# Modulation vectors of two transformer blocks: from VectorE sums to TensorE products in four column groups

## The reference

```python
# first block, layer l
ada = jax.nn.silu(c) @ w_ada[l] + b_ada[l]           # 1024 -> 6 * 1024
sh1, sc1, g1, sh2, sc2, g2 = jnp.split(ada, 6, axis=-1)
h = x * (1.0 + sc1) + sh1
y = mixer(h, ...)                                    # qkv, attention, w_o
x = layer_norm(ALPHA * x + (1.0 + g1) * y, ...)
h = x * (1.0 + sc2) + sh2
x = layer_norm(ALPHA * x + (1.0 + g2) * swiglu(h), ...)

# second block, layer l: two vectors from one matrix
mod_x = jax.nn.silu(c_2) @ w_ada_2[l] + b_ada_2[l]     # 1024 -> 9 * 1024
mod_c = jax.nn.silu(c_ctx_2) @ w_ada_2[l] + b_ada_2[l]
# swiglu half step, mixer, swiglu half step, each modulated and gated
```

## Time and profile before

| | |
|---|---|
| median of 3 runs | 2935.88 us (2933.57 to 2938.0) |
| the profiled execution | 2934.27 us |
| its span, first to last instruction | 2932.5 us |
| PE busy | 2669.5 us, 91% of the span |
| DVE busy | 1757.8 us, 60% |
| ACT busy | 1081.4 us, 37% |
| POOL busy | 224.9 us, 8% |
| read from HBM | 409.75 MB |
| mean granted clock of PE | 0.926 |

### The profile page before, as it was taken

How to read it: one execution, slowest core, us unless ns; L and a number is a source line. 1 busy time by engine, 2 the same in 40 slices (tenths; PEclk the granted TensorE clock), 3 DMA queues, 4 the chain that set the end, 5 groups by cost and what they waited for, 6 DMA issues and landing times. The chain is left out here.

```text
span 2932.5 us, 39627 instructions
## 1 busy us (share of the span) xinstructions
PE 2669.5 (91%) x15387; PEld 2241.6 (76%) x15387; DVE 1757.8 (60%) x3177; ACT 1081.4 (37%) x2061; POOL 224.9 (8%) x167
## 2 busy tenths in 40 slices
PE   4768998998998799998999889999899998988899
PEld 4747997867998588886855668888688886856899
DVE  6567776537776655545748566544655433647654
ACT  2343543433443323223326442322333322316553
POOL 2000100000100201101000020000111000100110
PEclk8867998967999899999989999999999999879999
DMA  8924774903676144332720134443244433720453
GB/s 287 279 84 144 254 255 130 270 29 102 232 243 200 51 150 144 126 122 83 214 72 1 44 100 130 137 133 119 93 145 135 138 120 116 214 72 24 142 178 133
DMA packets 355603, 413.91 MB, mean 141 GB/s; under 512 B 25707, under 2 KB 292628, under 8 KB 355352
## 3 DMA queue, kind: packets, MB, share of 16 engines
q1 hardware_dynamic: 353326, 404.37, 43.3%
q0 software_dynamic: 736, 4.58, 0.5%
q10 hardware_dynamic: 1354, 2.43, 0.2%
HBM read 409.75 MB, written 5.27 MB: 142 GB/s over the span
## 5 line engine op out<-in xcount | busy, mean ns | idle before, releaser
L640 DVE TENSOR_TENSOR weight_lo<-raw_weights,weight_hi 128x512 fp32r<-128x512 f32 x1024 | 778.1, 767 | 929.6 <-ACT weight_hi L1168 919.6
L1168 ACT ACTIVATE weight_hi<-raw_weights 128x512 fp32r<-128x512 f32 x1024 | 633.0, 629 | 1326.2 <-PE bank L845 1192.5
L845 PE MATMUL bank<-H_hi,weight_hi 128*128 128x256 f32 (+1 forms) x2832 | 975.0, 344 | 109.6 <-POOL H_lo L806 77.6
L845 PE MATMUL bank<-H_lo,weight_hi 128*128 128x256 f32 (+1 forms) x2832 | 956.4, 338 | 0.0
L845 PE MATMUL bank<-H_hi,weight_lo 128*128 128x256 f32 (+1 forms) x2832 | 956.4, 338 | 0.0
L845 PEld LDWEIGHTS bank<-H_hi,weight_hi 128*128 128x128 f32 x2832 | 558.0, 197 | 187.6 <-issue 112.6
L845 PEld LDWEIGHTS bank<-H_hi,weight_lo 128*128 128x128 f32 x2832 | 558.4, 197 | 50.7
L845 PEld LDWEIGHTS bank<-H_lo,weight_hi 128*128 128x128 f32 x2832 | 559.7, 198 | 48.7 <-issue 0.5
L1459 DVE SCALAR_TENSOR_TENSOR ada_partial<-raw_weights,silu_c,ada_partial 128x512 f32<-128x512 f32 x616 | 441.5, 743 | 1.3 <-DVE ada_partial L1459 0.2
L845 PE MATMUL bank<-hidden_hi,weight_hi 128*128 128x256 f32 (+1 forms) x1056 | 359.0, 340 | 3.8 <-DVE weight_lo L640 3.8
L845 PE MATMUL bank<-hidden_hi,weight_lo 128*128 128x256 f32 (+1 forms) x1056 | 354.1, 335 | 0.0
(11 more groups left out here) (165 smaller groups left out, 2124.4 us busy)
## 6 DMA issues: line engine op xcount, KB each, us to landing
raw_weights<-in_w_ada_dram SPq DMA_DIRECT2D x120, 1024.0 KB, 5.4
raw_weights<-in_w_ffn_up_dram SPq DMA_DIRECT2D x88, 1024.0 KB, 5.2
raw_weights<-in_w_ffn_in_dram SPq DMA_DIRECT2D x44, 1024.0 KB, 5.4
raw_weights<-in_w_ffn_down_dram SPq DMA_DIRECT2D x32, 1024.0 KB, 5.3
raw_weights<-in_w_in_dram SPq DMA_DIRECT2D x18, 1024.0 KB, 8.3
raw_weights<-in_w_ffn_out_dram SPq DMA_DIRECT2D x16, 1024.0 KB, 7.7
raw_weights<-in_w_in_ab_dram SPq DMA_DIRECT2D x12, 1024.0 KB, 9.4
raw_weights<-in_w_in_cd_dram SPq DMA_DIRECT2D x12, 1024.0 KB, 7.7
```

The source lines that it names most:

```text
L640: eng.tensor_tensor(WL[:, p.g % SPLIT, 0:p.kt * CW].rearrange("p (t n) -> p t n", n=CW), raw_ap(ch.n, ch.kt, CW)[:, p.k0:p.k0 + p.kt, :], ...
L845: return pe.matmul(o, w, x, start=start, stop=stop, skip_group_check=True)
L1168: act.activation(WH[:, p.g % SPLIT, 0:p.kt * CW].rearrange("p (t n) -> p t n", n=CW), raw_ap(ch.n, ch.kt, CW)[:, p.k0:p.k0 + p.kt, :], ACT ...
```

## The change

**PE does the products.** A chunk is used by PE alone: for each of its four row tiles one fp32 product with 512 moving columns of raw weights, straight from the slot. The stationary side is 32 columns wide, three conditioning vectors and 29 columns of zeros (`SILU_C`, now 128 by 8 by 32). Tile k writes partitions 32k to 32k + 31 of bank 7, so the four products of a chunk are in four column groups of the array. The second chunk of a group adds to the first.

**A group is then closed in three steps.** ACT copies the bank to `ada_sums` (`copy_sums`), at the second piece of the following main chunk. PE turns it by four transposes of 128 by 128 back into bank 7 (`turn_sums`), ahead of the last piece of that chunk. DVE adds the four partial sums by one small reduce and adds the bias (`join_sums`, `columns`), which counts `ada_out`. The first chunk of the next group waits for that count on PE.

**Chunks change places.** The first qkv hosts 8 instead of 12, the second 9 items instead of 8 (8 chunks instead of 7, since one item is not a main chunk), the third 7 instead of 8, and w_out of the second block's first layer 4 instead of none. Everything between is hosted four, later three, places later.

```diff
-        def ada(at, f):
-            close(f(at.u).raw_order)
-        def sum_rows(g):
-            nv = vectors(ADA[AG * g])
-            pe.wait_ge(ada_used, AG * (g + 1))
-            if g > 0:
-                pe.wait_ge(ada_out, g)
-            for j in range(AW // P):
-                for v in range(nv):
-                    ins = mm(B_ADA[:, j * nv + v:j * nv + v + 1],
-                             ACC[:, g % 2, v, j * P:(j + 1) * P], ones[:, 0:1], True, True)
-            ins.then_inc(ada_sum, 1)
+        def ada(ch):
+            wait_landed(pe, one, lambda _: ch)
+            g, first = ch.raw_order // AG, ch.raw_order % AG * AK
+            if first == 0 and g > 0:
+                pe.wait_ge(ada_out, g)
+            w = raw_ap(ch.n, AK, AW)
+            for k in range(AK):
+                ins = mm(B_ADA[32 * k:32 * k + 32, :], SILU_C[:, first + k, :], w[:, k, :], first == 0,
+                         first + k >= KC - AK)
+            ins.then_inc(ada_used, 1)
+            if first:
+                to_turn.append(g)
+        def turn_sums():
+            while to_turn:
+                g = to_turn.pop(0)
+                pe.wait_ge(ada_copied, g + 1)
+                for j in range(AW // P):
+                    ins = pe.transpose(B_ADA[:, P * j:P * j + P], ASUM[:, P * j:P * j + P], ident[:, :])
+                ins.then_inc(ada_sum, 1)
...
                 ins.then_inc(piece_used.sem, 1)
+                if i == len(ch.pieces) - 2:
+                    turn_sums()
...
+        def copy_sums():
+            while to_copy:
+                g = to_copy.pop(0)
+                act.wait_ge(ada_used, AG * (g + 1))
+                act.activation(ASUM[:, :], B_ADA[:, :], ACT.Copy).then_inc(ada_copied, 1)
...
-                    if first + k == 0:
-                        ins = dve.tensor_scalar(acc, w[:, k, :], SILU_C[:, i:i + 1], None, ALU.mult)
-                    else:
-                        chain.wait(closed["acc"][v])
-                        ins = dve.scalar_tensor_tensor(out=acc, in0=w[:, k, :], scalar=SILU_C[:, i:i + 1], in1=acc,
-                                                       op0=ALU.mult, op1=ALU.add)
...
+            parts = B_ADA[:, :].rearrange("p (c q r) -> p c r q", q=AK, r=32)[:, :, v0:v0 + nv, :]
+            chain.link(dve.tensor_reduce(APART[:, :, 0:nv], parts, AX.X, ALU.add))
+            dve.tensor_tensor(AD[m][:, n * at:n * at + n, 0:nv], APART[:, :, 0:nv],
+                              b[:, :, None].broadcast_to([P, n, nv]), ALU.add).then_inc(ada_out, 1)
...
 # proj, on DVE, after the eviction of a column group
                 dve.sem_inc(g.grp.tally.sem, 1)
+                join_sums()
+                if g.host:
+                    ada(g.host)
...
 # qkv, on DVE
-                    ahead_of(one, lambda _: it.chunk, (lambda _: it.host) if it.host else None)
+                    ahead_of(one, lambda _: it.chunk)
+                    join_sums()
+                    if it.host:
+                        ada(it.host)
...
-         (2816, ("v", 768))], T, 12, T, 0)
+         (2816, ("v", 768))], T, 8, T, 0)
...
-         (2560, ("v", 512)), (2816, ("v", 768))], T, 8, T, 1)
+         (2560, ("v", 512)), (2816, ("v", 768))], T, 9, T, 1)
...
-             (1280, ("k", 2)), (1536, ("v", 0)), (1792, ("v", 256)), (2048, ("kv",))], n, 8, T if last else n, 2 + l)
+             (1280, ("k", 2)), (1536, ("v", 0)), (1792, ("v", 256)), (2048, ("kv",))], n, 8 if last else 7, T if last else n, 2 + l)
...
-        w_out(a["w_out_2"][l], n2, 2 + l, 5, False, 0)
+        w_out(a["w_out_2"][l], n2, 2 + l, 5, False, 0 if last else 4)
```

More of the change, by code:

```diff
@@ L519, in qkv @@
         st.hosted = len(ADA)
+        assert st.hosted % AG == 0
         state.update(q_in=st.done, normed=None, hosted=st.hosted)
@@ L942, in qkv @@
                 if it.host:
-                    ada(one, lambda _: it.host)
-            if s.hosted:
-                close(s.hosted)
+                    ada(it.host)
+            turn_sums()
         def ffn_in(s):
@@ L1136, in _ @@
             elif s.kind == "ada":
+                pe.wait_ge(silu_done, 1)
                 for ch in s.chunks:
-                    ada(one, lambda _, ch=ch: ch)
-                close(s.hosted)
+                    ada(ch)
+                    turn_sums()
             elif s.kind in ("ln", "rms"):
+                turn_sums()
                 stats(s, before)
@@ L1200, in setup @@
             act.wait_ge(cols_done, 1)
[L1201 to L1204, removed]
+            for v in range(3):
+                ins = act.activation(SILU_C[:, :, v], C_COLS[:, 8 * v:8 * v + 8], ACT.Silu)
             ins.then_inc(silu_done, 1)
@@ L1263, in qkv @@
                     ahead(one, lambda _: p, split, late)
+                    if p is it.chunk.pieces[1]:
+                        copy_sums()
                 used(one, lambda _: it.chunk.pieces[-1])
@@ L1304, in step @@
                     ahead(at, lambda k: s.steps[k].u.pieces[i], split, late)
+                    if s.host and i == 1:
+                        ada(s.steps[at.u].host)
+                        copy_sums()
                 hidden_hi(at)
@@ L1397, in _ @@
             elif s.kind == "ada":
+                for ch in s.chunks:
+                    ada(ch)
+                    copy_sums()
                 flush()
@@ L1423, in _ @@
         late = list(range(SPLIT))
-        closed = {"read": 0, "acc": [0, 0]}
+        to_join = []
         one = At(None, 0, 1, 1)
@@ L1436, in used, with ada, ahead_of, join_sums @@
             dve.wait_ge(piece_used.sem, at(lambda s: f(s).g + SPLIT + 1))
[L1438 to L1454, removed]
-                    if first + k == 0:
-                        ins = dve.tensor_scalar(acc, w[:, k, :], SILU_C[:, i:i + 1], None, ALU.mult)
-                    else:
-                        chain.wait(closed["acc"][v])
-                        ins = dve.scalar_tensor_tensor(out=acc, in0=w[:, k, :], scalar=SILU_C[:, i:i + 1], in1=acc,
-                                                       op0=ALU.mult, op1=ALU.add)
[L1461 to L1469, removed]
-                ahead(at, lambda k: f(k).pieces[i], split, late)
[L1471 to L1477, removed]
+        def ada(ch):
+            if ch.raw_order % AG == AG - 1:
+                to_join.append(ch.raw_order // AG)
+        def ahead_of(at, f):
+            for i in range(len(f(at.u).pieces)):
+                ahead(at, lambda k: f(k).pieces[i], split, late)
+        def join_sums():
+            while to_join:
+                columns(to_join.pop(0))
         def columns(g):
@@ L1602, in step @@
                 dve.sem_inc(ev_dve.sem, 1)
[L1603 to L1606, removed]
-            else:
-                each(dve, 0, 10, 2, step)
-            step(At(None, 10, 1, 1))
+                if s.host:
+                    ada(s.steps[at.u].host)
+                    join_sums()
+            each(dve, 0, 11, 2, step)
         def proj(s):
@@ L1616, in proj @@
                 for ch in g.chunks:
-                    ahead_of(one, lambda _: ch, (lambda _: g.host) if g.host and ch is g.chunks[-1] else None)
+                    ahead_of(one, lambda _: ch)
                 used(one, lambda _: g.chunks[-1].pieces[-1])
@@ L1778, in _ @@
             elif s.kind == "ada":
+                lambdas()
                 for ch in s.chunks:
-                    ada(one, lambda _, ch=ch: ch)
-                    if ch is s.chunks[3]:
-                        lambdas()
-                close(s.hosted)
+                    ada(ch)
+                    join_sums()
                 flush()
```

46 lines of the change are left out of this document (26 added, 20 removed).

## The result

The changed kernel takes **3038.58 us** (median of 4 runs, 3035.18 to 3042.28), the kernel before, run beside it, 2936.94 (2933.57 to 2939.59): ratio **1.0347, 95% interval 1.0328 to 1.0366**, 101.6 us slower. The forecast was 3039.

A forecast was written before the change was run, and what follows sets the result against it. PE, 91% busy, was taken to bind most, with DVE's work mostly hidden. Terms 83 - 12 + 31 + 12 - 4 - 12 + 3 + 2 = +103 us on 2934.27 gave 3039 us (median 1.6 above); own range 2976 to 3065, stated range 2965 to 3090.

The forecast's parts named there:

- PE's price: Where PE is full: 1.2 us per chunk, 0.6 per group, +156 us; sum blocks leaving PE -73; net +83.
- Four groups side by side: Modulation products on PE: four column groups run fully side by side, as two do in attention; 1.06 us per block.
- The rival of two at a time: Modulation products on PE: pairs go one after the other, sum rises by 90 us to 3129; chance 0.09.
- Strict order: Rival: second records wait for first in PE's queue, four products take five record times; +135 us, 3174; chance 0.04.
- The new wait: PE waits for DVE's join: 3.7 and 4.0 us in projections (+31), 2.0 in qkv (+12), second qkv -4.
- eight projections ... +31: One wait of PE for the join in each of eight projections, 3.7 or 4.0 us each: +31 us.
- What DVE gives back: DVE loses its sums; gain is 2.2 us in each of 5.5 step pairs at 750 to 870 us: -12.
- Worth something only where DVE binds: DVE's relief counts at 750 to 870 us, -12, and in the second qkv at most 6.8 us.
- First qkv and setup: First qkv: -12 for three items without modulation, +3 for the nine before; setup +2, between -3 and +8.
- What would show it: Signs in the new trace, among them the first k,q product 10 us earlier than 160.96 and join waits of 43 to 60.
- ACT gets 60 copies ... hidden: ACT's 60 bank copies, 0.63 us each, are hidden, since ACT has 69 us of work in 140.
- Second qkv: Three join waits come where PE waited for pieces anyway (6.8 us); both put together at -4.

The follow-up runs named there:

- the experiment with two groups: Changed kernel with DVE's join one piece earlier (2970.84 us), a chunk's four products put in two column groups instead of four: 3050.95 us.
- the small one alone: Kernel before with only the four chunks moved and open groups closed behind each projection, sums still on DVE: 2911.24 us, ratio 0.9927.

## Why the prediction was right, step by step

- *PE's price.* Right where PE is fullest: 1.2 us per chunk against 1.23 in the up stages, measured by leaving the products out. Too high in the projections, 0.87. A pair of steps with 512 columns 1073.38 - 1026.90 = 46.48 against 46.5 forecast; with 256 columns and two vectors 785.13 - 759.25 = 25.88 against 26.0 (starts of two chunks' products, two steps apart).
- *Four groups side by side.* Shown. The rival of two at a time is the experiment with two groups, 80 us away; the 0.09 that it had was fair, since no row of the kernel before had shown more than two. Strict order fell too: the four first records start within 0.02 us (1166.254 to 1166.274), the second ones 0.45 later, and two records of one product take as long as eight of four. The estimate by the Trainium skill ("TensorE: Matmul & The Clock Gate", Part 3, measured speedup) of 1.08 us for the block is 0.08 above the 1.00 to the next main product.
- *The new wait.* Mechanism and place right, size wrong in one of two parts. The projections' waits, forecast at 3.7 and 4.0, are 3.6 to 3.9, eight of them; qkv's, forecast at 2.0, are 1.87 to 1.90; 53.4 us in all within 43 to 60. But I priced a wait at its own length: "eight projections ... +31" recovered 49.6 when it went. The clock behind the pause was missing, 18.4 us by the estimate above. The forecast for the projections holds all the same (55.4 against 59.5), since other terms there missed the other way.
- *What DVE gives back.* Half counted. "Worth something only where DVE binds", -12, was near for the second up stage (13.9 with the sums out, 10.4 of it behind the first 96 products), and left out 3.8 in the first w_out, 4.0 in the second down-projection, 5.6 in the first qkv and 7.5 in the setup. I read DVE's shortage in one stretch of the earlier trace rows and did not look at the stages next to it. Either half of the change alone gives the second up stage's gain of 7.8 or nearly so.
- *First qkv and setup.* Forecast -12 + 3 + 2, measured -5.0. The first k,q product moved from 160.96 to 156.9, by 4 us, not the 7 of these terms (the 10 under "What would show it" does not follow from them). The step that failed is "ACT gets 60 copies ... hidden": I argued it from stretches where the pieces were in place, and in this one the copy stood behind a rounding that waited for its load, 8.75 us. With the copy moved ahead it is -7.9 at once.
- *Second qkv.* Forecast +4.6 by its terms, measured +6.9; that the waits for the join would coincide with the waits for pieces held only in part.

That the total hit within 1 us is luck in part. In the projections it is 19 us more for the clock against 15 less elsewhere. Of the 15, DVE's relief is 7.8 (first w_out, second down): PE's wait for the evictions behind the first w_out is 0.7 us where it was 5.3, so that stage is 9.7 us longer to its last main product and only 4.1 to the next stage. The rest is about what the chunks there cost less than 1.2 us, 26 x 0.33 = 8.6. In the up-projections it is 7 less, of which 4.0 lie in the first 96 products of the first and the second (granted clock 0.63 and 0.70, where it was 0.57 in both before); in the first two stages 2 more.

## What to carry to other kernels

Before moving work off an engine, price what its relief is worth by leaving the work out: here about 44 us, against 123 for its new place on the engine that was full. A change of two parts is two experiments, since the small one alone was the gain, and it was worth 24 us only with the sums on DVE. When an engine's queue gets a hand-over to wait for, put the other engine's small step ahead of its next big one, and ahead of anything that waits for a load; one call placed a piece earlier gave 68 us.

## What the chip showed that I had not expected

- Four fp32 products of 128x32 weights and 512 columns in four column groups take 1.06 us, one takes 1.04: the three others are free to within the trace's reading.
- A pause of 3.6 to 3.9 us on PE was followed by the lower clock in all eight cases (granted clock 0.69 to 0.85 over the ten us from its end; seven times the block itself took 1.93 to 1.94 us instead of 1.07). Nine pauses of 1.9 us in the later qkv stages left it at 1.00. The eight longer ones lasted 30 us together, and 49.6 came back without them.
